# Sample's paged key scores four sequences at a time, with re-placed value buffers and five joined edits, in a two-layer hybrid decoder step

## The chip, the cores and the metric

The kernel is one program of several stages on one core of one Trainium2 chip. The metric is the device time of one execution in microseconds. TensorE (PE in the profile) multiplies and transposes; VectorE (DVE), ScalarE (ACT) and GpSimd (POOL) do the elementwise work; SyncE (SP) mostly asks for transfers. Each engine runs its own list of instructions in order, and they wait for one another on semaphores.

## The reference

Two layers run over 1024 prompt tokens and over 8 sample sequences of 4 new tokens each. The odd layer's sparse attention is the part that the change touches most. For a sample sequence it scores 8 query heads (in 2 key groups of 4) against the 1024 past keys, which lie in 8 pages of 128 keys, found by a page table:

```python
def _dsa_sample(q, k, v, qi, wi, ki, layer, cache_k, cache_v, cache_ik, page_table):
    ...
    kg = _paged_take(cache_k, layer, page_table, idx, k)
    vg = _paged_take(cache_v, layer, page_table, idx, v)
    return _sparse_attend(q, kg, vg, valid)
```

`_sparse_attend` is a masked softmax of q·k over the chosen keys times v. The kernel scores all keys and masks those that were not chosen. The even layer ends with a gMLP branch, `u * mixed * silu(gate)` for tiles of 128 tokens, and both layers end with an output projection that is added to the input.

## The kernel before

The stages follow one another: the even layer's front with its branches (0 to about 752 us), its output projection (to 917), the odd layer's front with indexer and selection (to 1522.75), and the odd layer's back, `layer1_back` (to the end). In each stage a plan, a list of slots written out by hand, sets the order: `follow` goes through the slots and, for each engine apart, advances the streams named in the slot by one step.

In `layer1_back` the streams are called in a slot in the order `smp`, `prep`, `job`, `ties` (for PE, `prep` issues the transposes of a block's queries and keys). `job` runs in slots 0 to 66: 64 jobs, one for each of 8 blocks of 128 prompt queries and 8 heads. A job is scores on PE (`scores`, `back_s` in the profile, up to 1024 keys wide, so 128 columns for the first eight jobs and 1024 for the last eight), mask and maximum on DVE (L4323), exponentials on ACT (L4203), transposes of the probabilities on PE (`all_banks`, L4060), their copy on ACT or DVE (L4198 on ACT), and the product with the values on PE (L4069). `prep` makes the queries and keys of block p (p = 2 is block 1 of the prompt and begins in slot 1; p = 3 to 8 are blocks 2 to 7 and begin in slots 6, 14, 22, 30, 38 and 46): ACT squares (L4156), DVE reduces (L4252), POOL takes the root and multiplies and rotates (L3874 and the lines after it), PE transposes (L3953).

`smp` is Sample. Slots 1 to 17 are its paged key scores, in 16 units. Unit u is four key pages of one sequence. SP asks for three of the four pages and POOL for the fourth, into a ring of four key buffers. PE transposes the pages of the two key groups (`turned`, L3968, eight transposes into the banks `bankX` and `bankZ`), ACT copies one bank (L4175) and DVE the other (L4273) to `skT`, a ring of two, and PE multiplies (`smp_scores`, L3980): two products of 512 columns with 128 stationary columns. `qz` is the queries laid out with zeros in all columns but the 32 of this sequence, so that four units add into one bank `bankY` without disturbing one another. After each four units DVE adds the mask rows (`ye`). In slot 18 the scores against the four new keys follow (L3997). The softmax over all of it and its transposes (L4008) come next, and from slot 23 on the products with the value pages (L4031), four matmuls a page. The value pages of eight sequences go through a ring of four buffers `vp`, asked for by POOL (b = 0 to 4 and 6) and SP (5 and 7); those of b = 4 and 5 may be asked for only when the products of the first pair of sequences are done (`pvd`).

POOL starts the stage with `minus` and `qz` cleared (L3856, L3858) and then asks for its key pages; ACT may lay out `qz` only after that (`made`, L4145). At a stage's end `clear` resets the stage's semaphores in barriers of all engines, one for each run of adjacent numbers (L84). In the output projections the fp32 weights are split into an upper part (ACT, L351) and the rest (DVE, L395), and PE takes three products for each piece. At the even layer's end DVE does `mixed` (L2163, four pieces) and `gated` (L2170) for each tile of the gMLP; u and the gate come back from memory (`gu`, `gg`), except the gate of the last tile, which is taken from the evacuation's buffer `st`. L1760 is the evacuation itself.

## Time and profile before

| | |
|---|---|
| three runs | 1963.12 us median, 1958.63 to 1963.51 |
| the profiled execution | 1961.93 us, span 1960.3 us, mean granted clock 0.972 |
| PE busy | 1823.4 us, 93% of the span |
| DVE, ACT, POOL busy | 975.5, 601.6, 421.3 us |
| `layer1_back`, 1522.75 to 1960.30 | 437.55 us, of which PE is busy 394.89 |

PE is busy for most of the time in every stage, so an edit can gain where PE waits or where it takes work from PE. The rows further down give the places. "Idle before" in square brackets is the time that the engine stood still ahead of a row, and what ended it.

### The profile page before, as it was taken

What the parts mean: (1) busy time and instruction counts of PE and PEld (TensorE: products, weight loads), DVE (VectorE), ACT (ScalarE), POOL (GpSimd) and SP (SyncE); (2) the same over time, 40 slices, a digit from 0 to 9 for tenths busy, and PEclk for the clock granted to TensorE, in tenths of its full rate; (3) what the DMA queues carried; (4) which work ended last, traced back from release to release, by engine and by line L of the source; (5) the groups of instructions that cost most, each with busy time, mean ns of one, the idle gap of its engine ahead of it and who ended that gap; (6) DMA issues with size and microseconds to landing.
All of it is one profiled execution on the core that took longest, in us unless ns stands there. A gap on an engine that the chain in (4) does not pass through costs nothing. (4 is left out here: it accounts for less than half of the span.)

```text
span 1960.3 us, 26802 instructions
## 1 busy us (share of the span) xinstructions
PE 1823.4 (93%) x9553; PEld 1407.4 (72%) x9553; DVE 975.5 (50%) x2274; ACT 601.6 (31%) x1273; POOL 421.3 (21%) x663
## 2 busy tenths in 40 slices
PE   7999999999999997998999898999989689899998
PEld 5666788777777885886876466787667466677887
DVE  5412643224466765123431567888776555575211
ACT  3111332111122113101211346787634345453000
POOL 4301222000133442000331001211004364430000
PEclk9999999998899998999999999999999899999999
DMA  6433333444344467122222121334243755323221
GB/s 210 136 108 113 104 109 108 157 159 126 105 140 155 127 201 292 76 101 79 65 66 69 42 71 61 113 100 148 99 144 90 233 171 151 123 87 98 105 113 44
DMA packets 128487, 235.15 MB, mean 120 GB/s; under 512 B 28354, under 2 KB 54370, under 8 KB 128354
## 3 DMA queue, kind: packets, MB, share of 16 engines
q1 hardware_dynamic: 109010, 170.63, 26.8%
q0 software_dynamic: 18144, 58.47, 9.5%
q10 hardware_dynamic: 1200, 4.33, 0.6%
q8 instruction: 77, 1.26, 0.3%
q14 instruction: 56, 0.46, 0.1%
HBM read 167.22 MB, written 66.16 MB: 119 GB/s over the span
## 5 line engine op out<-in xcount | busy, mean ns | idle before, releaser
L1170 PE MATMUL layer_acc<-layer_w_hi,layer_xT_hi 128*128 128x512 f32 x640 | 262.7, 410 | 0.2 <-PE all_banks L1318 0.2
L1172 PE MATMUL layer_acc<-layer_w_hi,layer_xT_lo 128*128 128x512 f32 x640 | 253.9, 397 | 0.0
L1171 PE MATMUL layer_acc<-layer_w_lo,layer_xT_hi 128*128 128x512 f32 x640 | 253.2, 396 | 0.0
L2726 PE MATMUL front_acc<-front_w_hi,front_xT_hi 128*128 128x512 f32 x520 | 221.3, 426 | 16.2 <-DVE front_st L3196 5.2
L2727 PE MATMUL front_acc<-front_w_lo,front_xT_hi 128*128 128x512 f32 x520 | 208.9, 402 | 0.0
L2728 PE MATMUL front_acc<-front_w_hi,front_xT_lo 128*128 128x512 f32 x520 | 208.6, 401 | 0.0
L1170 PEld LDWEIGHTS layer_acc<-layer_w_hi,layer_xT_hi 128*128 128x128 f32 x640 | 122.4, 191 | 30.6 <-issue 5.9
L1171 PEld LDWEIGHTS layer_acc<-layer_w_lo,layer_xT_hi 128*128 128x128 f32 x640 | 121.7, 190 | 26.8 <-issue 2.6
L1172 PEld LDWEIGHTS layer_acc<-layer_w_hi,layer_xT_lo 128*128 128x128 f32 x640 | 121.3, 189 | 27.0
L2726 PEld LDWEIGHTS front_acc<-front_w_hi,front_xT_hi 128*128 128x128 f32 x520 | 100.5, 193 | 49.5 <-issue 7.9
L3042 ACT ACTIVATE front_index_rows<-odd_bias,front_candidate 128x1024 bf16<-128x1024 f32 (+3 forms) x128 | 124.9, 981 | 14.3 <-DVE front_candidate L3336 9.3
L2728 PEld LDWEIGHTS front_acc<-front_w_hi,front_xT_lo 128*128 128x128 f32 x520 | 99.4, 191 | 23.7
L2727 PEld LDWEIGHTS front_acc<-front_w_lo,front_xT_hi 128*128 128x128 f32 x520 | 100.4, 193 | 17.2
L2554 POOL DMA_DIRECT2D all_w<-in_w_odd x57 | 32.7, 574 | 318.2 <-DVE front_w_lo L3244 120.3
L996 POOL DMA_DIRECT2D all_w<-in_w_even x80 | 44.7, 560 | 260.9 <-DVE layer_w_lo L109 139.5
L1526 ACT ACTIVATE layer_st<-layer_acc 128x512 f32<-128x512 f32 x48 | 28.7, 597 | 228.8 <-PE layer_acc L1172 222.5
L4069 PEld LDWEIGHTS all_banks<-back_v,back_first_scratch 128*128 128x128 f32 x576 | 73.6, 198 | 33.8 <-issue 25.8
L4069 PE MATMUL all_banks<-back_v,back_first_scratch 128*128 128x128 f32 x576 | 80.1, 286 | 17.9 <-issue 13.9
L1524 ACT ACTIVATE layer_st<-layer_acc 128x512 f32<-128x512 f32 (+1 forms) x36 | 21.5, 597 | 227.8 <-PE layer_acc L1172 224.5
L301 PE MATMUL out_acc<-out_w_hi,out_yT_hi 128*128 128x512 f32 x192 | 77.0, 401 | 11.7 <-DVE out_w_lo L395 11.7
L4203 ACT ACTIVATE back_first_scratch<-back_first_scratch,back_neg 128x128 f32<-128x128 f32 (+7 forms) x64 | 49.8, 779 | 109.3 <-DVE back_neg L4329 60.1
L4046 PE MATMUL back_s<-back_kT,back_first_scratch 128*128 128x512 f32 (+3 forms) x192 | 74.3, 497 | 8.3 <-ACT back_kT L4139 8.3
(661 smaller groups left out, 3680.8 us busy)
## 6 DMA issues: line engine op xcount, KB each, us to landing
all_w<-in_w_even POOLq DMA_DIRECT2D x80, 256.0 KB, 3.8
h_even<-layer_st SPq DMA_DIRECT2D x79, 256.0 KB, 2.1
all_w<-in_w_odd POOLq DMA_DIRECT2D x61, 256.0 KB, 3.6
h_odd<-front_st SPq DMA_DIRECT2D x56, 256.0 KB, 2.1
layer_scratch<-h_even SPq DMA_DIRECT2D x47, 256.0 KB, 3.0
all_scratch<-in_w_mem SPq DMA_DIRECT2D x32, 256.0 KB, 3.9
all_scratch<-h_even SPq DMA_DIRECT2D x32, 256.0 KB, 3.7
all_scratch<-x SPq DMA_DIRECT2D x14, 512.0 KB, 3.6
```

The source lines that it names most:

```text
L301: T.matmul(out, yh[u][:, k, :], wh[:, k, e], start=(k == 0), stop=False, skip_group_check=True)
L996: pool.dma_start(raw[n % RAW][:, :], a["w_even"][ORDER[chunk][0] // CW, :, CW * kk:CW * kk + CW]).then_inc(w_in[n % RAW], 16)
L1170: T.matmul(out[0:rows, :], xh[:, kk, to], wh[:, r, :], start=(kk == 0), stop=False)
L1171: T.matmul(out[0:rows, :], xh[:, kk, to], wl[:, r, :], start=False, stop=False)
L1172: ins = T.matmul(out[0:rows, :], xl[:, kk, to], wh[:, r, :], start=False, stop=(kk == KC - 1))
L2726: T.matmul(out[0:rows, :], xh[:, k, to], wh[:, r, :], start=(k == 0), stop=False, skip_group_check=True)
L2727: T.matmul(out[0:rows, :], xh[:, k, to], wl[:, r, :], start=False, stop=False, skip_group_check=True)
L2728: ins = T.matmul(out[0:rows, :], xl[:, k, to], wh[:, r, :], start=False, stop=(k == KC - 1), skip_group_check=True)
L3042: A(flags_at(i), rows_at(i), ACT.Sign, bias=cand[:, j:j + 1], scale=-1.0, accum_out=cnt[:, j:j + 1]).then_inc(ca, 1)
L4046: T.matmul(psS[:, 512 * (m % 2):512 * (m % 2) + n], qT[i % 2][:, h, :], kT[:, h // 4, k:k + n], start=True, stop=True)\
L4069: ins = T.matmul(bankO[:, 0:P], pT[g % 2][:, k, :], v[:, k, HD * (h // 4):HD * (h // 4) + HD], start=(k == 0), stop=(k == i))
L4203: A(y, y, ACT.Exp, bias=neg[g % 3][:, :], scale=SC, accum_out=tot[g % 4][:, :]).then_inc(ex, 1)
```

## The change

1. **Scores by four.** `smp_scores` runs only after the units 3, 7, 11 and 15, for four units at once: eight products, each with the 32 stationary columns of its own sequence, into four column tiles `bankY[32q:32q+32]`. `turned` still runs for every unit. The ring `skT` has six places.
2. **Pages.** SP asks for two key pages and POOL for two on even units (three and one on odd ones). Each of the eight value buffers has a place of its own until the fourth pair, where two places are used again. ACT now asks for the value pages of b = 0 and 1, one page at the end of each of the first 16 job slots; POOL asks for b = 2 in slots 13 to 16; b = 3, 4 and 5 are asked for in slots 17 to 20 by SP and POOL; b = 6 and 7 in slot 27 (the fifth w step), after the first pair's products. At the stage's start POOL asks for three key pages (units 2 and 3) before its memsets, SP asks for unit 2's pages and the first gate tile earlier, and eight small transfers of Sample's gate (`gs`) go from the start to slots 13 and 14. ACT copies the keys before the queries and lays out `qz` in slot 1.
3. **Prep later.** For p > 2 the DVE reduction and POOL's steps come one slot after ACT's square.
4. **Last output tile.** Its products run by halves of 512 columns; sum and store follow each half.
5. **One range.** The last stage clears its semaphores in one barrier.
6. **First weight piece.** In the even layer's output projection the first piece is split in two halves.
7. **gMLP's end.** The tile before the last (i = 7) also takes its gate from `st` and has its u loaded early, and DVE takes `mixed` 7, `gated` 7 and `mixed` 8 ahead of tile 6.

```diff
+    def clear_range(self):
+
+        self.nc.all_engine_barrier(sems_to_clear=range(min(self.nums), max(self.nums) + 1))
+
...
             def w_upper(k):
                 act.wait_ge(*w_there(k))
+                if k == 0:
+                    for e in halves:
+                        A(wh[:, k, e], w(k)[:, e], ACT.Copy).then_inc(whi, 1)
+                    return
                 A(wh[:, k, :], w(k), ACT.Copy).then_inc(whi, 1)
...
             def w_lower(k):
-                dve.wait_ge(whi, k + 1)
+                if k == 0:
+                    for n, e in enumerate(halves):
+                        dve.wait_ge(whi, n + 1)
+                        V.tensor_tensor(wl[:, k, e], w(k)[:, e], wh[:, k, e], ALU.subtract).then_inc(pieces, 1)
+                    return
+                dve.wait_ge(whi, k + 2)
                 V.tensor_tensor(wl[:, k, :], w(k), wh[:, k, :], ALU.subtract).then_inc(pieces, 1)
 
...
-        u_of = lambda i: X[:, 512:1024] if i == T1 - 1 else gu[i % 2]
+        u_of = lambda i: X[:, 512:1024] if i == T1 - 1 else S[:, 3072:3584] if i == T1 - 2 else gu[i % 2]
+        late_gate = lambda i: i >= T1 - 2
...
-                sp.wait_ge(gyd, i + 1)
+                sp.wait_ge(gyd, T1 - 1 if i == T1 - 3 else i + 1)
...
-                    if i == 6:
+                    if i == 5:
                         load_gu(T1 - 1)
+                        load_gu(T1 - 2)
...
                 u, rows = i % 2, rows_in(TILE[i])
-                gate = gg[u] if i < T1 - 1 else st[(UNITS - 1) % ST]
+                gate = st[(UNITS - T1 + i) % ST] if late_gate(i) else gg[u]
                 V.tensor_tensor(u_of(i)[0:rows, :], u_of(i)[0:rows, :], gate[0:rows, :], ALU.mult).then_inc(gyd, 1)
...
                 for i in range(T1):
-                    if i:
+                    if i == T1 - 2:
+                        mixed(T1 - 2)
+                        dve.wait_ge(*evacuated(UNITS - 2))
+                        gated(T1 - 2)
+                        mixed(T1 - 1)
+                    if 0 < i < T1 - 1:
                         mixed(i - 1)
                         gated(i - 1)
                     if i + 2 < T1:
                         norm(i + 2)
-                    if i == T1 - 1:
-                        mixed(T1 - 1)
                     yield
...
-        skT = [WH[:, 4096 + 1024 * u:5120 + 1024 * u].rearrange("p (n k) -> p n k", n=KVH) for u in range(2)]
+        skT = [(WH[:, 4096 + 1024 * u:5120 + 1024 * u] if u < 2 else WL[:, 2048 + 1024 * u:3072 + 1024 * u]).rearrange("p (n k) -> p n k", n=KVH)
+               for u in range(TRING)]
...
-        vp = [WL[:, 2048 * r:2048 * r + 2048].rearrange("p (g n) -> p g n", g=PAGES) for r in range(VRING)]
+        vp = [of[:, at:at + 2048].rearrange("p (g n) -> p g n", g=PAGES) for of, at in (
+            (WL, 0), (WL, 2048), (WH, 0), (WH, 2048), (WL, 4096), (WL, 6144), (WL, 0), (WL, 2048))]
+        by_pool = lambda u: (2, 3) if u % 2 == 0 else (3,)
...
+                load_last_k(2)
+                load_last_k(3)
                 G.memset(minus[:, :], -SC).then_inc(made, 1)
                 pool.wait_ge(made, 1)
                 G.memset(qz, 0.0).then_inc(made, 1)
-                load_last_k(2)
-                load_last_k(3)
...
-                        if step == 0:
+                        at = step - (p > 2)
+                        if at == 0:
                             pool.wait_ge(red, p - 1)
...
+                for p in by_pool(u):
+                    at = PAGES * seq_of(u) + 4 * hf + p
+                    page = pool.value_load(c.page_ids[0:1, at:at + 1], min_val=0, max_val=n_pool - 1)
+                    src = a["cache_attn_k"][0, bass.ds(page, 1)].rearrange("o s h d -> (o s) (h d)")
+                    pool.dma_start(kp[r][p], src).then_inc(kq_in[r], 16)
...
 
             def smps():
                 for u in range(UNITS + 6):
                     if u + KRING < UNITS:
                         load_last_k(u + KRING)
-                    if 2 <= u < UNITS + 2:
...
+                    pe.wait_ge(kp_in[r], 16 * (4 - len(by_pool(u))) * loads)
+                    pe.wait_ge(kq_in[r], 16 * len(by_pool(u)) * loads)
                 else:
-                    pe.wait_ge(qcp, 2)
+                    pe.wait_ge(qcp, 3)
...
-            def smp_scores(u):
-                gr, hf, q = unit(u)
-                pe.wait_ge(kca, u + 1)
-                pe.wait_ge(kcd, u + 1)
-                if u == 0:
+            def smp_scores(m):
+                pe.wait_ge(kca, 4 * m + 4)
+                pe.wait_ge(kcd, 4 * m + 4)
+                if m == 0:
                     pe.wait_ge(qcp, 6)
-                if q == 0:
-                    pe.wait_ge(ye, u // 4)
+                pe.wait_ge(ye, m)
                 for n in range(KVH):
-                    ins = T.matmul(bankY, qz[:, n, seq_of(u), :], skT[u % 2][:, n, :], start=(q == 0 and n == 0), stop=(q == 3 and n == 1),
-                                   skip_group_check=True)
+                    for q in range(4):
+                        u, e = 4 * m + q, slice(32 * q, 32 * q + 32)
+                        ins = T.matmul(bankY[e, :], qz[:, n, seq_of(u), e], skT[u % TRING][:, n, :], start=(n == 0), stop=(n == 1),
+                                       skip_group_check=True)
                 ins.then_inc(sc2, 1)
...
@@ -4170,9 +4223,9 @@
             def smps():
                 for u in range(UNITS):
                     act.wait_ge(ktr, 2 * u + 1)
-                    if u >= 2:
-                        act.wait_ge(sc2, u - 1)
-                    A(skT[u % 2][:, 0, :], bankX, ACT.Copy).then_inc(kca, 1)
+                    if u >= TRING:
+                        act.wait_ge(sc2, (u - TRING) // 4 + 1)
+                    A(skT[u % TRING][:, 0, :], bankX, ACT.Copy).then_inc(kca, 1)
...
+                    if g < 2 * PAGES:
+                        b, p = divmod(g, PAGES)
+                        act.dma_start(vp[b][:, p, :], value_page(act, b, p)).then_inc(va_in[b], 16)
                     yield
...
-                        if step == 0:
+                        if step == (0 if p == 2 else 1):
                             dve.wait_ge(squ, p - 1)
                             link(V.tensor_reduce(ssq[u][0:rows, :], heads(sq[0:rows, :], H10), AX.X, ALU.add))
...
-                            dve.wait_ge(sc2, u - 1)
-                        V.tensor_copy(skT[u % 2][:, 1, :], bankZ).then_inc(kcd, 1)
+                        if u >= TRING:
+                            dve.wait_ge(sc2, (u - TRING) // 4 + 1)
+                        V.tensor_copy(skT[u % TRING][:, 1, :], bankZ).then_inc(kcd, 1)
                     if u and u % 4 == 0:
                         gr, hf, _ = unit(u - 1)
-                        dve.wait_ge(sc2, u)
+                        dve.wait_ge(sc2, u // 4)
...
+                if j == T1 - 1:
+                    for n, e in enumerate(HALVES):
+                        dve.wait_ge(mm, j + n + 1)
+                        V.tensor_tensor(x[u][:, e], psS[:, e], x[u][:, e], ALU.add).then_inc(add, 1)
+                    return
```

The next two excerpts are PE's program in the units 3 and 4 of Sample (`back_first_smp` and `all_w` are the key pages; in the L3980 row and in the L4022 row `back_first_smp` is the turned keys and `qz`). Before:

```order
L3980 MATMUL back_x<-back_first_smp 128x512 x2
L4069 MATMUL all_banks<-back_v,back_first_scratch 128x128
L4060 MATMUL all_banks<-all_ident,back_first_scratch 128x128
L4046 MATMUL back_s<-back_kT,back_first_scratch 128x128
L3968 MATMUL back_x<-all_ident,back_first_smp 128x128 x4
L3968 MATMUL all_banks<-all_ident,back_first_smp 128x128 x4
L3980 MATMUL back_x<-back_first_smp 128x512 x2
L4069 MATMUL all_banks<-back_v,back_first_scratch 128x128
L4060 MATMUL all_banks<-all_ident,back_first_scratch 128x128
L4046 MATMUL back_s<-back_kT,back_first_scratch 128x128
```

And PE in the same slots after the change:

```order
L4010 MATMUL back_x<-all_ident,back_first_smp 128x128 x4
L4010 MATMUL all_banks<-all_ident,back_first_smp 128x128 x4
L4113 MATMUL all_banks<-back_v,back_first_scratch 128x128
L4104 MATMUL all_banks<-all_ident,back_first_scratch 128x128
L4090 MATMUL back_s<-back_kT,back_first_scratch 128x128
L4010 MATMUL back_x<-all_ident,all_w 128x128 x4
L4010 MATMUL all_banks<-all_ident,all_w 128x128 x4
L4022 MATMUL back_x<-back_first_smp 32x512 x8
L3995 MATMUL all_banks<-all_ident,all_scratch 128x128 x4
L4113 MATMUL all_banks<-back_v,back_first_scratch 128x128
L4104 MATMUL all_banks<-all_ident,back_first_scratch 128x128
L4090 MATMUL back_s<-back_kT,back_first_scratch 128x128
```

The two products of 512 columns that followed each unit's eight transposes are gone, and eight products with 32 stationary columns stand once behind four units.

The following two are POOL's program at the start of `layer1_back` (each TENSOR_LOAD reads a page number, each DMA asks for one key page). Before:

```order
L3856 MEMSET back_minus_scale 128x1
L3858 MEMSET back_first_smp 128x2048
L3895 TENSOR_LOAD odd_pages
L3895 ISA x2
L3897 ISA
L3897 DMA back_first_smp<-in_cache_attn_k 128x256
L3895 TENSOR_LOAD odd_pages
L3895 ISA x2
L3897 ISA
L3897 DMA back_first_smp<-in_cache_attn_k 128x256
L3862 MEMSET back_own 128x16
L3866 MEMSET back_own 32x1 x8
```

And POOL at that place after the change:

```order
L3938 TENSOR_LOAD odd_pages
L3938 ISA x2
L3940 ISA
L3940 DMA back_first_smp<-in_cache_attn_k 128x256
L3938 TENSOR_LOAD odd_pages
L3938 ISA x2
L3940 ISA
L3940 DMA back_first_smp<-in_cache_attn_k 128x256
L3938 TENSOR_LOAD odd_pages
L3938 ISA x2
L3940 ISA
L3940 DMA back_first_smp<-in_cache_attn_k 128x256
L3899 MEMSET back_minus_scale 128x1
L3901 MEMSET back_first_smp 128x2048
```

The memset of `qz` (128x2048) now stands behind three page requests instead of ahead of the first.

The last two are DVE's program at the end of the even layer (L1760 evacuates, L2163 is `mixed`, L2170 `gated`, 17 lines further down in the changed file). Before:

```order
L1760 SCALAR_TENSOR_TENSOR layer_st<-layer_st,layer_acc 128x512
L2163 SCALAR_TENSOR_TENSOR layer_scratch<-layer_a,layer_bs,layer_scratch 128x128 x4
L2170 TENSOR_TENSOR layer_scratch<-layer_scratch 128x512
L1760 SCALAR_TENSOR_TENSOR layer_st<-layer_st,layer_acc 128x512
L2163 SCALAR_TENSOR_TENSOR layer_scratch<-layer_a,layer_bs,layer_scratch 128x128 x4
L2170 TENSOR_TENSOR layer_scratch<-layer_scratch 128x512
L2163 SCALAR_TENSOR_TENSOR all_scratch<-all_banks,layer_bs,all_scratch 128x128 x4
L2170 TENSOR_TENSOR all_scratch<-all_scratch,layer_st 128x512
```

And DVE after the change:

```order
L2180 SCALAR_TENSOR_TENSOR layer_scratch<-layer_a,layer_bs,layer_scratch 128x128 x4
L2187 TENSOR_TENSOR layer_scratch<-layer_scratch,layer_st 128x512
L2180 SCALAR_TENSOR_TENSOR all_scratch<-all_banks,layer_bs,all_scratch 128x128 x4
L2180 SCALAR_TENSOR_TENSOR layer_scratch<-layer_a,layer_bs,layer_scratch 128x128 x4
L2187 TENSOR_TENSOR layer_scratch<-layer_scratch 128x512
L1777 SCALAR_TENSOR_TENSOR layer_st<-layer_st,layer_acc 128x512
L2187 TENSOR_TENSOR all_scratch<-all_scratch,layer_st 128x512
```

The last evacuation now has one multiplication of 128x512 behind it, where it had two groups of `mixed` and two of `gated`.

## Rows read from the trace of the kernel before

**Rows 1.** The page's busy times: engine, us, share of the span, instructions.
```profile
PE 1823.4 (93%) x9553; PEld 1407.4 (72%) x9553; DVE 975.5 (50%) x2274; ACT 601.6 (31%) x1273; POOL 421.3 (21%) x663
```

**Rows 2.** Windows: length, PE, PEld, DVE, ACT, POOL busy, PE clock, DMA share, GB/s.
```profile
1524.10:1543.70 19.60, 13.54 (x61) 9.56 (x61) 9.95 (x25) 7.02 (x34) 8.95 (x21) 0.85 0.93 314
1543.70:1574.50 30.80, 25.09 (x113) 16.27 (x113) 24.51 (x64) 11.34 (x30) 13.54 (x15) 0.88 0.68 202
1574.50:1604.10 29.60, 27.17 (x144) 18.46 (x144) 14.05 (x47) 12.71 (x32) 17.09 (x26) 1.00 0.60 184
```

**Rows 3.** Timeline of PE, slots 1 to 18: start, length, row, idle before.
```profile
1532.43 0.66 PE L3968 MATMUL back_x<-all_ident,back_first_smp 128*128 128x128 f32 x4 [2.01 <-DMA back_first_smp<-in_cache_attn_k]
...
1574.55 0.63 PE L3968 MATMUL back_x<-all_ident,back_first_smp 128*128 128x128 f32 x4 [1.60 <-ACT back_first_smp L4175]
...
1575.45 1.88 PE L3980 MATMUL back_x<-back_first_smp 128*128 128x512 f32 x4
1577.17 0.61 PE L4069 MATMUL all_banks<-back_v,back_first_scratch 128*128 128x128 f32 x4
...
1604.06 3.63 PE L3997 MATMUL back_x<-back_kT,back_first_smp 128*128 128x4 f32 x32
```

**Rows 4.** Timeline of PE in the even layer, a group in column tiles.
```profile
352.54 0.64 PE L1318 MATMUL all_banks<-layer_scratch 128*32 128x256 f32 x8
```

**Rows 5.** Timeline at the start of `layer1_back`, POOL, ACT and DVE.
```profile
1522.90 1.81 POOL L3858 MEMSET back_first_smp<- 128x2048 f32 x1
...
1524.74 1.34 ACT L4145 ACTIVATE back_first_smp<-all_banks 128x16 f32<-128x16 f32 x16 [0.61 <-POOL back_first_smp L3858]
...
1528.22 1.49 DVE L4252 TENSOR_REDUCE all_scratch<-all_scratch 128x10 f32<-128x1280 f32 x1 [0.81 <-ACT all_scratch L4156]
...
1537.03 0.55 POOL L3907 DMA_DIRECT2D back_first_smp<-in_cache_attn_v  x1 [0.60 <-PE all_banks L3968]
...
1541.70 0.35 DVE L4339 SCALAR_TENSOR_TENSOR all_mem_keysT<-all_banks,back_rec,all_mem_keysT 128x128 f32<-128x128 f32 x1 [4.13 <-DMA all_mem_keysT<-h_odd]
```

**Rows 6.** Groups of instructions of DVE and of ACT, 1524 to 1605 us.
```profile
L4273 DVE COPY back_first_smp<-all_banks 128x512 f32<-128x512 f32 x16 | 11.1, 691 | 7.7 <-PE all_banks L3968 6.9 <-DVE odd_bias L4360 0.4
L4175 ACT ACTIVATE back_first_smp<-back_x 128x512 f32<-128x512 f32 x16 | 9.4, 590 | 2.4 <-PE back_x L3968 2.4
```

**Rows 7.** Timeline of PE where the value products wait, and after.
```profile
1669.78 0.63 PE L4031 MATMUL back_x<-back_first_smp 128*16 128x128 f32 x16 [3.61 <-DMA back_first_smp<-in_cache_attn_v]
1670.34 2.10 PE L4069 MATMUL all_banks<-back_v,back_first_scratch 128*128 128x128 f32 x10
...
1675.99 1.28 PE L4069 MATMUL all_banks<-back_v,back_first_scratch 128*128 128x128 f32 x10
```

**Rows 8.** Timeline of PE and DVE where a block is prepared.
```profile
1627.05 1.20 PE L4069 MATMUL all_banks<-back_v,back_first_scratch 128*128 128x128 f32 x4 [2.97 <-issue]
...
1651.55 1.49 DVE L4252 TENSOR_REDUCE all_scratch<-all_scratch 128x10 f32<-128x1280 f32 x1 [1.20 <-ACT all_scratch L4156]
...
1718.82 2.90 PE L4069 MATMUL all_banks<-back_v,back_first_scratch 128*128 128x128 f32 x12 [2.29 <-issue]
```

**Rows 9.** Timeline of DVE at the even layer's end.
```profile
745.93 0.69 DVE L1760 SCALAR_TENSOR_TENSOR layer_st<-layer_st,layer_acc 128x512 f32<-128x512 f32 x1 [2.09 <-ACT layer_st L1524]
748.08 1.13 DVE L2163 SCALAR_TENSOR_TENSOR layer_scratch<-layer_a,layer_bs,layer_scratch 128x128 f32<-128x128 f32 x4 [1.46 <-DMA layer_scratch<-h_even]
...
751.00 0.69 DVE L2170 TENSOR_TENSOR all_scratch<-all_scratch,layer_st 128x512 f32<-128x512 f32 x1
```

**Rows 10.** Timeline of DVE, the first weight piece of the output projection.
```profile
755.55 1.23 DVE L395 TENSOR_TENSOR out_w_lo<-all_scratch,out_w_hi 128x1024 fp32r<-128x1024 f32 x1 [0.25 <-ACT out_w_hi L351]
```

**Rows 11.** Timeline of DVE, the last sum.
```profile
1953.51 1.23 DVE L4388 TENSOR_TENSOR all_scratch<-back_s,all_scratch 128x1024 f32<-128x1024 f32 x1 [15.10 <-PE back_s L4117]
```

**Rows 12.** Waits of SP's queue, 1945 to 1961 us: sum, times, longest.
```profile
SPq L84 <- PEq L84: 2.0, 3, 0.8
```

**Rows 13.** Timeline of ACT, its own page requests' nearest relative.
```profile
798.08 1.46 ACTq L356 DMA_DIRECT2D x<-all_scratch  x2
```

158 lines of the change are left out of this document (90 added, 68 removed).

## The prediction

> **What bounds it now.** I read the page's busy times first: PE is busy for 93% of the span [rows 1], so a gain is either work taken from PE or a place where PE stands still. Then the table by stretch, which shows where that is. In the 80.0 us of Sample's paged scores PE is busy 13.5 of 19.6, 25.1 of 30.8 and 27.2 of 29.6 us [rows 2]. Each stretch has its own limit. In the second DVE is busy 24.5 of 30.8 us, and PE's clock was granted at 0.85 and 0.88. In the third PE itself is full, at full clock. Last, PE's timeline says who ends its waits: key pages at 1532.43, ACT's copy at 1574.55 [rows 3], value pages for 3.61 us at 1669.78 [rows 7], and the copy behind a block's preparation (up to 2.97 us, released by nothing that the profile names) at 1627.05 and 1718.82 [rows 8].
>
> **What an edit of PE's work is worth.** One unit's two products begin at 1575.45 and the next work at 1577.17: 1.72 us, and 1.88 to their own end, so 0.16 of draining [rows 3]. Sixteen units are 27.5 us. For column tiles the nearest row is the even layer's: four products of 256 columns in tiles of 32 take 0.64 us [rows 4]. One after the other the same 1024 columns are the 1.88 us of a unit. Less the drain that is 0.48 against 1.72, so tiles run 3.6 times as fast, nearly side by side. Eight products of 512 columns are then two rounds of 0.86 plus about 0.14, **1.85 us**; if the shorter product's overhead doubles with its length, 2 x 2 x 0.48 = 1.9 and the drain, 2.1; if tiles don't overlap, 8 x 0.86 = 6.9. Four calls at 1.85 are 7.4, so PE loses 20.1 us of work (0 where tiles don't overlap). The Trainium skill ("TensorE: Matmul & The Clock Gate", Measured speedup vs the span model) gives 2.38 times for three column tiles of 512; for four at that efficiency an estimate is 3.2 times, 2.2 us a call, which would make the sum smaller by at most 1.3 us.
>
> **Slots 1 to 17, -12.5 us.** Not all 20 us come out, because PE isn't the limit everywhere.
> - *Start.* POOL now makes three page requests ahead of the memset of 1.81 us. A request is 0.55 us and 0.60 of reading the page number, 1.15 [rows 5], so the memset ends 3.45 later. ACT's layout of `qz` (1.34) waits for it, the square stands behind that, and DVE's reduction, now at 1528.22, comes at 1531.7 at the latest. On the other side PE's wait of 2.01 us for pages at 1532.43 [rows 3] goes.
> - *Up to `turned(10)`, now at 1574.55.* DVE has 9.95 + 24.51 = 34.5 us of work in these two stretches [rows 2]. Laid end to end from 1531.7 it is done at 1566.2. About 2.8 us of it is exchanged for waits that the chain mask, exponential, transposes, sum keeps: **1569**, a gain of 5.5. The wait of 4.13 us at 1541.70 for the gate tile [rows 5] ends because SP asks for it first; it is part of the slack that these 5.5 use up. The bounds are 0 (the late start eats it all) and 8.3 (no waits).
> - *Slots 11 to 17.* From 1574.55 to 1604.06 are 29.5 us with seven units' products [rows 3]. Seven go (12.0) and two calls of 1.85 come: 21.2. ACT is busy 12.71 there and now has up to seven page requests; DVE 14.05, POOL 17.09 [rows 2]. A request by ACT is 0.73, from 1.46 for two [rows 13], so ACT has 17.8 of 21.2 us. It fits, closely. I give 1.4 us back for places where ACT or POOL is late, so Sample's last scores come at **1591.5** and not 1604.06. Bounds -5 and -20 (all of PE's work).
> - *Copies.* ACT's copy of a unit takes 0.59 and DVE's 0.69 us [rows 6], the same number as before. The ring of six lets them run ahead, which costs nothing and saves no time of theirs.
>
> A rule speaks against the size of this. The Trainium skill ("TensorEngine Tiling (Array Packing)", PSUM Bottleneck) says that after a fourfold speedup of TensorE the copy out of PSUM may become the limit. By it the gain would stay at some 3 us; that case stands among the rivals, worked out from rows.
>
> **Value pages, -5.4.** Before, POOL and SP could ask for sequences 4 and 5 only after the first pair's products, and PE stood 3.61 us at 1669.78. Behind this wait the same ten products took 2.10 us where they take 1.28 a little later [rows 7], which is PE's clock at half; with the transposes and scores of that slot in the same ratio this is about 1.8. Now pages of 4 and 5 are asked for in slots 17 to 20, far ahead, and those of 6 and 7 in slot 27, with the second, third and more slots of other work over them. What hides them is the jobs of a slot, over 4 us each; without that cover a pair is the 3.61 again. Bounds -3.6 and -6.
>
> **Prep later, -5.5.** DVE waits for ACT's square (1.20 us at 1651.55, then 1.49 for the reduction [rows 8]), and the job's mask stands behind it, so PE idles. There are four such slots (22, 30, 38, 46): the first idles PE 2.97, the last 2.29, and the last one's products then run 2.90 us at a lower clock [rows 8]. With the square a slot earlier the 1.2 or more of DVE's wait goes each time and the 1.49 of the reduction stays: four times about 1.2, and 0.7 for the clock. What is late next is POOL, whose rotation must be ready for PE's transposes at step 6: it begins one slot later with the same room behind, about a slot. Bounds -2 and -10.
>
> **Even layer's end, -4.3.** DVE's last evacuation is done at 745.93 + 0.69 = 746.6, then it waits 1.46 for u and gate of tile 7 and ends at 751.69 [rows 9]. Now only one multiplication of 0.69 stands behind the evacuation: 747.3. The stage change follows DVE, so 4.4; I take 4.3. If stores or PE take over, 3; bounds -3 and -4.8.
>
> **First piece, -1.0.** DVE's half of 1.23 [rows 10] is 0.69, as 128x512 rows of DVE are [rows 9], so 0.54; ACT's copy ahead of it is halved too, an estimate of 0.45. Bounds 0 and -1.2.
>
> **Tail, -1.9.** The last sum of 1.23 [rows 11] ends in a half of 0.69, 0.54 less. Of the barriers' 2.0 us in three waits [rows 12] a third stays, 1.3 less. Bounds -1.2 and -2.6.
>
> **The sum.** 12.5 + 5.4 + 5.5 + 4.3 + 1.0 + 1.9 = 30.6. Against the profiled execution's 1961.93 that is 1931.3; its own time lies 1.2 below the runs' median 1963.12, so I forecast **1932.5 us** for the median.
>
> **Rivals.**
> - *Chain-bound slots (0.12).* The hand-overs of a job between PE, DVE and ACT, with the copies of 0.59 and 0.69, set the slots and not PE's work. Then the first ten slots gain nothing and slots 11 to 17 give 3: 12.5 becomes 3, **1942**. For it: DVE 24.5 of 30.8. Against: PE 27.2 of 29.6 in the third stretch [rows 2].
> - *Tiles don't overlap (0.07).* Eight products cost 6.9. Slots 11 to 17 gain nothing and the first part half: some 2, **1943**. Against it stands the 0.64 [rows 4].
> - *More (0.05).* DVE's waits vanish, the clock comes up from 0.85 and 0.88, and the four prep slots lose all their idle time: slots 1 to 17 give 18, prep 9: 1923, and less with each bound.
> - *Slower (0.04).* ACT's 16 page requests, with an address from a register, are dear. ACT is busy 31.1 us in the 80.0 [rows 2], and everything in its list waits behind a request. With price p its work is 31.1 + 16p. The other terms give 18.1, so it decides above 98.1 us, p = 4.2. At p = 5 it is 111.1, 31.1 more than now: **1976**. For it: nothing here shows such a request by ACT. Against it: two plain ones take 1.46 [rows 13], and POOL's, with the page number, 1.15 each [rows 5].
> - *No change (0.02).* All these places are hidden by something that I don't see, and the late start takes the rest: 1963.
>
> **How the numbers follow.** The forecast has 0.70. Its own terms' bounds give 1920 to 1948; not all ends come together, so 1922 to 1943. With chain-bound slots and tiles that don't overlap, whose own spread reaches 1946, the range is **1920 to 1946**. Within 0.3% (6 us, about what a measurement of this kernel can tell from none) is 1957 to 1969: faster 0.94, same 0.02, slower 0.04.
>
> **What would show it.** the scores against the four new keys (L3997 before) at about 1586 us on the profile's clock (1591.5 less the 5.3 gained in the stages before) and not 1604; the row of eight products at some 2 us; ACT's requests under 1 us; no wait of L4031 for value pages; the stage `layer1_back` near 412 us where it is 437.55; PE's idle time in slots 22, 30, 38 and 46 at half or less; DVE's last row of the even layer ending near 747. I would be wrong if DVE or ACT shows as the releaser of PE in slots 11 to 17, or if PE's transposes of a block wait for POOL's rotation.

## The result and the profile after

The changed kernel takes 1934.43 us (median of 4 runs, 1932.26 to 1936.03), the one before 1961.13 (4 runs, 1958.63 to 1963.51). The ratio is 0.9863, 95% interval 0.9846 to 0.9879: 26.7 us less. The forecast was 1932.5 us, worked out as 30.6 less than the profiled execution; the two profiled executions differ by 29.6 in span (1930.7 against 1960.3). The sum came out, but partly by chance: its largest term came to half, another was too small, and 1.9 us came from stages that nothing touched.

The windows of the changed kernel over the same three stretches of Sample's scores, counted from the stage's first ACT row (columns as in [rows 2]):

```profile
1517.50:1537.10 19.60, 10.63 (x49) 9.54 (x48) 9.42 (x23) 6.64 (x32) 9.70 (x21) 0.56 0.95 329
1537.10:1567.30 30.20, 20.14 (x122) 13.37 (x123) 24.89 (x66) 12.39 (x32) 12.32 (x13) 0.80 0.64 198
1567.30:1594.20 26.90, 25.07 (x177) 19.74 (x178) 14.62 (x50) 13.36 (x34) 15.69 (x21) 0.91 0.74 232
```

PE does less in the first two (10.6 and 20.1 us where [rows 2] has 13.5 and 25.1), and its clock fell from 0.85 and 0.88 to 0.56 and 0.80. PE's timeline there, with the rows that answer to [rows 3]:

```profile
1523.21 1.09 PE L4010 MATMUL back_x<-all_ident,all_w 128*128 128x128 f32 x4 [3.17 <-ACT back_first_smp L4228]
1524.09 1.06 PE L4010 MATMUL all_banks<-all_ident,all_w 128*128 128x128 f32 x4
1529.55 1.09 PE L4010 MATMUL back_x<-all_ident,back_first_smp 128*128 128x128 f32 x4 [3.76 <-ACT back_first_smp L4228]
...
1540.86 3.64 PE L4022 MATMUL back_x<-back_first_smp 128*32 128x512 f32 x16
...
1558.41 1.92 PE L4022 MATMUL back_x<-back_first_smp 128*32 128x512 f32 x16
...
1567.25 1.09 PE L4010 MATMUL back_x<-all_ident,back_first_smp 128*128 128x128 f32 x4 [4.21 <-ACT back_first_smp L4228]
...
1590.84 3.63 PE L4040 MATMUL back_x<-back_kT,back_first_smp 128*128 128x4 f32 x32
```

The eight products in column tiles take 1.92 us, as sized (1.85), and 3.64 where the clock is at half (1.2 instead of 2.4 GHz). A group of four transposes takes 1.06 instead of 0.60 for the same reason. The waits of PE from 1517 to 1800 us name who ends them (us in total, times, longest):

```profile
PE back_x L4010 <- ACT back_first_smp L4228: 16.2, 7, 4.2
...
PE all_banks L4113 <- ACT back_first_scratch L4251: 6.2, 8, 1.6
PE all_banks L4113 <- issue: 3.9, 3, 1.8
```

In the same view of the kernel before, PE waited 3.6 us for that copy; now 16.2. No value page is among the releasers (3.61 in [rows 7]). What ACT does ahead of such a copy, on its timeline:

```profile
1527.70 0.40 ACT L4256 ACTIVATE back_first_scratch<-back_first_scratch,back_neg 128x128 f32<-128x128 f32 x1 [2.15 <-DVE back_neg L4383]
1528.01 0.19 ACT L4256 ACTIVATION_READ_ACCUMULATOR back_first_scratch<-back_first_scratch,back_neg 128x1 f32 x1
1528.40 0.36 ACTq L4266 DMA_DIRECT2D back_first_smp<-in_cache_attn_v  x1
1528.81 0.60 ACT L4228 ACTIVATE back_first_smp<-back_x 128x512 f32<-128x512 f32 x1 [0.61 <-issue]
```

The exponential waits for DVE's mask, then comes the page request, and only then the copy: 0.61 us of standing still, and PE's transposes at 1529.55 wait behind it.

DVE's timeline has at the even layer's end the rows that answer to [rows 9] and [rows 10], and at the start of the last stage its first mask:

```profile
746.45 0.69 DVE L1777 SCALAR_TENSOR_TENSOR layer_st<-layer_st,layer_acc 128x512 f32<-128x512 f32 x1 [2.55 <-ACT layer_st L1541]
747.17 0.69 DVE L2187 TENSOR_TENSOR all_scratch<-all_scratch,layer_st 128x512 f32<-128x512 f32 x1
...
751.38 1.28 DVE L405 TENSOR_TENSOR out_w_lo<-all_scratch,out_w_hi 128x512 fp32r<-128x512 f32 x2
...
1520.60 0.29 DVE L4379 CUSTOM_DVE_ANT_0 back_first_scratch<-back_s,odd_bias 128x128 f32<-128x128 f32 x1 [7.99 <-POOL back_minus_scale L3899]
...
1545.68 0.35 DVE L4395 SCALAR_TENSOR_TENSOR all_mem_keysT<-all_banks,back_rec,all_mem_keysT 128x128 f32<-128x128 f32 x1 [0.33 <-DVE back_rec L4390]
```

PE's timeline has the first product behind them:

```profile
752.21 0.77 PE L305 MATMUL out_acc<-out_w_hi,out_yT_hi 128*128 128x512 f32 x1 [6.43 <-DVE out_w_lo L405]
```

And SP's waits at the kernel's end answer to [rows 12]:

```profile
SPq L77 <- PEq L77: 1.1, 1, 1.1
```

DVE ends the even layer at 747.86 (751.69 in [rows 9]). Its first mask in the last stage waits for POOL's small memset, which now stands behind three page requests. And the wait of 4.13 us for the gate tile [rows 5] is gone: the same row at 1545.68 waits for no transfer.

**A measure that is steadier than the total.** Between two marks that no edit moves in any run, from the first product of the even output projection to the first ACT row of `layer1_back`, the runs took 762.0 to 768.4 us. The first mark scatters too: 749.9 to 755.0 us in the eleven traces with the changed even layer, 756.9 to 757.6 in the three without. So I read the stage by itself: times from its first ACT row to DVE's copy of unit 10 (the eleventh), to Sample's scores against the new keys, and to the last job's reciprocal on DVE, each worked out from timeline rows. The same code in three runs gave 53.0, 52.9 and 53.1 us, then 74.7, 74.5 and 74.6, and in two runs 253.1 and 253.0 for the last. The ratios are against executions of the kernel before taken beside each group of runs, whose medians are in its row.

| kernel | unit 10 | new scores | last job | median of runs | ratio to before, interval |
|---|---|---|---|---|---|
| before | 52.9 | 81.3 | 273.7 | 1961.13 to 1962.64 | |
| changed | 53.0 | 74.7 | 253.1 | 1934.43 | 0.9863, 0.9846 to 0.9879 |
| page request before exponential | 50.6 | 71.3 | 251.0 | 1931.87 | 0.9847, 0.9816 to 0.9878 |
| scores of each unit | 49.2 | 76.3 | 255.8 | 1936.23 | 0.9875, 0.9843 to 0.9907 |
| POOL's memsets first | 51.9 | 73.7 | 253.8 | 1932.15 | 0.9848, 0.9822 to 0.9874 |
| preparation together | 55.2 | 81.0 | 270.7 | 1953.45 | 0.9951, 0.9928 to 0.9974 |
| units, then fours | 49.0 | 69.3 | 249.0 | 1932.93 | 0.9855, 0.9827 to 0.9884 |
| before, preparation later | 48.9 | 81.3 | 267.9 | 1956.79 | 0.9967, 0.9945 to 0.999 |
| value pages late | 53.1 | 74.6 | 259.3 | 1941.9 (one run) | |
| ends as before | 52.9 | 74.5 | 253.0 | 1940.21 | 0.9885, 0.9858 to 0.9912 |
| first pages by POOL | 49.0 | 78.0 | 260.6 | 1941.69 | 0.9898, 0.9868 to 0.9927 |
| useless products | 49.7 | 70.1 | 249.7 | 1930.09 | 0.9845, 0.9808 to 0.9882 |
| fours late, small memset first | 48.3 | 68.2 | 249.2 | 1929.52 | 0.9841, 0.9814 to 0.9869 |
| first pages by SP | 49.8 | 75.2 | 254.7 | 1935.1 | 0.9865, 0.9838 to 0.9892 |

(In the expectations below, "to the transposes of unit 10" was read from PE's rows, about 1 us ahead of DVE's copy. The 48.1 of products of each unit is that row; the 52.4 named for the run with the request moved is the row of unit 11, and that of unit 10 is 49.5.)

### The profile page after: what moved, and what is told of

Read it like the earlier page. It is cut to its first block and busy times, and to the rows that moved or that the text cites. A ratio compares the mean times of both kernels' runs of the same rounds, so it can differ in the third digit from the quotient of the medians.

```text
span 1930.7 us, 26765 instructions
## 1 busy us (share of the span) xinstructions
PE 1802.3 (93%) x9553; PEld 1396.5 (72%) x9553; DVE 977.6 (51%) x2276; ACT 602.7 (31%) x1274; POOL 412.5 (21%) x646
## 5 line engine op out<-in xcount | busy, mean ns | idle before, releaser
L1189 PE MATMUL layer_acc<-layer_w_hi,layer_xT_lo 128*128 128x512 f32 x640 | 253.8, 397 | 0.0
L1189 PEld LDWEIGHTS layer_acc<-layer_w_hi,layer_xT_lo 128*128 128x128 f32 x640 | 121.4, 190 | 27.1
L4113 PEld LDWEIGHTS all_banks<-back_v,back_first_scratch 128*128 128x128 f32 x576 | 71.3, 194 | 23.7 <-issue 13.0
L4256 ACT ACTIVATE back_first_scratch<-back_first_scratch,back_neg 128x128 f32<-128x128 f32 (+7 forms) x64 | 49.7, 776 | 97.2 <-DVE back_neg L4385 56.2
```

The lines of the kernel that those rows point to most:

```text
L1189: ins = T.matmul(out[0:rows, :], xl[:, kk, to], wh[:, r, :], start=False, stop=(kk == KC - 1))
L4113: ins = T.matmul(bankO[:, 0:P], pT[g % 2][:, k, :], v[:, k, HD * (h // 4):HD * (h // 4) + HD], start=(k == 0), stop=(k == i))
L4256: A(y, y, ACT.Exp, bias=neg[g % 3][:, :], scale=SC, accum_out=tot[g % 4][:, :]).then_inc(ex, 1)
```

## The experiments

**ACT's request ahead of the exponential.**

```diff
+                    if g < 2 * PAGES:
+                        b, p = divmod(g, PAGES)
+                        act.dma_start(vp[b][:, p, :], value_page(act, b, p)).then_inc(va_in[b], 16)
                     if g < JOBS:
                         exps(g)
-                    if g < 2 * PAGES:
-                        b, p = divmod(g, PAGES)
-                        act.dma_start(vp[b][:, p, :], value_page(act, b, p)).then_inc(va_in[b], 16)
```

> The changed kernel with ACT's value-page request moved ahead of the job's exponential, where ACT waits for DVE's mask anyway. Theory: in slots 1 to 10 a chain goes round once per slot, from PE's scores over DVE's mask, ACT's exponential and ACT's copy of the turned keys (L4228, for which PE waits 16.2 us in 7 waits) back to PE's next transposes, and the request (0.6 to 0.85 us between exponential and copy) lies in it. Then some 7 x 0.6 = 4 us come out between the stage's first ACT row and Sample's last scores (74.7 us now, about 71 then), and the kernel takes about 1930 us. Rival: ACT comes too late for the mask anyway, so the place of the request is worth nothing and the stretch stays within 1 us of 74.7.

New scores 3.4 us earlier, the last job 2.1. On ACT the copy now starts 0.40 us after its exponential (1529.75 and 1530.15), where it was 1.11. The request was in the chain; the theory held.

**Products of each unit.** `smp_scores` as before the change, all else as changed.

```diff
-                    if u % 4 == 3:
-                        smp_scores(u // 4)
+                    smp_scores(u)
```

> The changed kernel with the products of each unit as before, two of 512 columns with 128 stationary ones after each unit's transposes; everything else of the change stays (ring of six, pages, start). Theory: the first ten slots are bound by the chain through DVE and ACT, so that the 1.72 us of products are hidden there (0 to 1 us), and slots 11 to 17 by PE, where 7 x 1.72 - 2 x 1.92 = 8.2 us of work come back and about 6 of it shows. In all 6 to 7 us slower than the changed kernel, the stretch to Sample's last scores 81 us instead of 74.7. Rival A: PE's work is what binds in all slots, then 4 x (4 x 1.72 - 1.92) = 20 us. Rival B: the chain binds in all slots and the gain there came from the pages and the ring, then 0 to 2 us.

Neither the theory's 6 to 7 nor rival A: 1.6 us later at the new scores, 2.7 at the last job (by DVE's reciprocals 4.6 from the 19th to the 46th job; that 1.9 come back at the 47th I did not follow up). The 1.6 lies in rival B's range, but not for its reason, since PE's work does bind in slots 11 to 17. With 20 us more of products on PE in all 16 units the first ten slots are 3.8 us *shorter* (49.2 against 53.0), and from there to the new scores it is 27.1 against 21.7. The first two windows of this kernel:

```profile
1516.70:1536.30 19.60, 14.47 (x61) 9.99 (x60) 10.33 (x25) 7.20 (x34) 9.70 (x21) 0.73 0.96 329
1536.30:1566.50 30.20, 24.72 (x124) 16.26 (x125) 25.25 (x68) 13.13 (x35) 15.11 (x18) 0.97 0.73 223
```

The clock is at 0.73 and 0.97 where fours have 0.56 and 0.80.

**POOL's memsets first.**

```diff
+                G.memset(minus[:, :], -SC).then_inc(made, 1)
+                pool.wait_ge(made, 1)
+                G.memset(qz, 0.0).then_inc(made, 1)
                 load_last_k(2)
                 load_last_k(3)
-                G.memset(minus[:, :], -SC).then_inc(made, 1)
-                pool.wait_ge(made, 1)
-                G.memset(qz, 0.0).then_inc(made, 1)
```

> The changed kernel with POOL's two memsets ahead of its three key page requests, as before the change. DVE's first mask waits for the first memset now and starts 4.4 us after the stage's first ACT row, 2.4 before the change. Theory: this late start is carried into the chain of the first slots and costs 1 to 2 us, so 1 to 2 us faster than the changed kernel. Rival: the key pages of unit 2 then come late and PE waits up to 2.0 us for them as before the change, so nothing is gained or 1 us lost.

1.0 us at the new scores, given back by the last job (0.7 later). The order at the start is worth nothing in the end.

**Preparation together again.**

```diff
-                        at = step - (p > 2)
+                        at = step
...
-                        if step == (0 if p == 2 else 1):
+                        if step == 0:
```

> The changed kernel with DVE's reduction and POOL's steps of a block's preparation in the same slot as ACT's square, as before the change. Theory: the four slots 22, 30, 38 and 46 lose again what the two traces show as gained there, 3.2 + 1.6 + 1.1 + 2.7 = 8.6 us, and slots 6 and 14 some tenths: 7 to 9 us slower than the changed kernel. The forecast had 5.5 for it. Rival: most of these steps came from other edits (gate transfers moved, value pages asked for elsewhere), then 0 to 3 us.

17.6 us in the stage, 17 by the two ratios: twice the theory and three times the forecast. 6.3 of it is there at the new scores already. DVE's reciprocals, one for each job, say where: 7.8 us are lost by the 18th job, that is with blocks 2 and 3, whose preparation begins in slots 6 and 14, and 9.8 in the four slots behind (4.5, 1.6, 1.0 and 2.7). PE's waits in this kernel, 1520 to 1790 us:

```profile
PE back_x L4010 <- ACT back_first_smp L4228: 15.5, 8, 3.8
PE all_banks L4113 <- issue: 15.3, 7, 3.0
```

The waits of the jobs' value products that nothing in the profile ends ("issue") are 15.3 us where the changed kernel has 3.9 (13.9 before).

**Units first, then fours**, with the request moved.

```diff
-                    if u % 4 == 3:
-                        smp_scores(u // 4)
+                    if u < 8:
+                        smp_scores(u)
+                    elif u % 4 == 3:
+                        smp_scores_of_four(u // 4)
```

> The kernel with ACT's page request ahead of the exponential, and the products of units 0 to 7 as before (each unit by itself, 128 stationary columns), of units 8 to 15 by fours in column tiles. Theory after the first four runs: with the products gone PE does so little in the first ten slots that its clock is granted lower (0.56 and 0.80 of full speed in the two stretches with fours, 0.73 and 0.97 with each unit's products), the transposes take 1.06 instead of 0.60 us, and the chain gets longer by what PE's other work loses. Then both halves are had: the first ten slots as with each unit (48.1 us from the first ACT row to the transposes of unit 10, or a little less by the moved request), then 23.6 us as with fours: Sample's last scores 68 to 71 us after the first ACT row, where the fours with the moved request took 71.3 and the changed kernel 74.7. In all 2 to 5 us faster than the changed kernel. Rival: the clock has nothing to do with it, the extra 8 x 1.72 us of PE work cost what they cost, and the stretch is 73 us or more.

69.3 us to the new scores, as expected: 5.3 us before the changed kernel. 4.1 of it arrive at the last job.

**The kernel before, preparation later.** The two edits of the fourth run the other way round, in the kernel before.

> The kernel before with one part of the change alone: DVE's reduction and POOL's steps of a block's preparation one slot after ACT's square, for p > 2. Undoing this in the changed kernel cost 17.6 us of the stage. Theory: it is worth about as much by itself, since the square's wait stands in front of a job's mask on DVE whatever else is done: 10 to 17 us faster than before. Forecast: 5.5 us faster. Rival: in the kernel before, other waits take its place (gate tile, value pages), then 0 to 3 us.

5.7 us in the stage and 5.8 in the medians (2 to 11 by the interval): near the forecast's 5.5, and not the theory's 10 to 17. Up to unit 10 it gains 4.0, and all of that is lost by the new scores. PE's row in slot 12 says where:

```profile
1581.99 1.12 PE L3954 MATMUL all_banks<-all_ident,all_scratch 128*128 128x128 f32 x4 [4.14 <-POOLq L3888]
```

PE waits 4.14 us for POOL's rotation of block 2. The step that is moved later runs into POOL's page requests. So the 5.7 is a difference: by DVE's reciprocals this kernel is 1.8 us behind at the 18th job, and gains 7.6 behind it, where the four slots lie that the forecast priced. Sample's value pages still keep PE waiting, only earlier: 3.86 us at 1656.03, where the kernel before waits 3.61 at 1669.78.

**Value pages late.**

```diff
-                    if UNITS <= u < UNITS + 4:
-                        load_v(4, range(2 * (u - UNITS), 2 * (u - UNITS) + 2))
...
                     if w == 4:
                         pool.wait_ge(pvd, 1)
-                        load_v(6, range(PAGES))
+                        load_v(4, range(PAGES))
+                    if w == 8:
+                        load_v(6, range(PAGES))
```

> The changed kernel with the value pages of sequences 4 and 5 asked for only after the products of the first pair, those of 6 and 7 four slots later, as before the change (POOL and SP as now, places as now). Theory: PE waits for them again for some 3.6 us before the third pair's products and then runs at a lower clock for a slot: 5 us more between the 32nd and the 34th job's end (7.4 us now, 12.7 before the change). Rival: POOL has less to do in those slots than before, so the pages are asked for earlier and the wait is under 1 us.

The last job comes 6.2 us later, and PE waits again ahead of the value products:

```profile
PE back_x L4073 <- issue: 3.8, 1, 3.8
```

The cost stands between the jobs 27 and 33 rather than at the 33rd, since the stage is ahead by then (0.6 us at the 17th job); the size is the forecast's (5.4, bounds 3.6 to 6), a little above.

**Ends as before.** Even layer's end, first piece, last tile and clearing undone together (their hunks of the diff reversed).

> The changed kernel with the even layer's end, the split first weight piece, the last output tile by halves and the one-range clearing undone. Theory: the first product of the even layer's output projection starts 4.7 us later (756.9 instead of 752.2), and the time behind the last job grows by 2.5 us (163.9 instead of 161.4): 7.2 us in all. Between the two traces 1.9 us more were gained in the stages from 752 to 1516 us, in which nothing was changed; the rival to chance is that this hangs on the earlier start, and then it is 9 us.

The first product of the output projection starts at 757.6 us (752.2 changed, 756.9 before), and the time behind the last job is 162.9 (161.4 and 163.9). That is 5.4 and 1.5 us. The 5.4 is a difference of single traces; the means of the eleven and the three traces named above differ by 4.9. Of the tail's 1.5, the last sum is 0.5 (1.22 against 0.69), the landing of the last store 0.6 (SP waits 2.2 against 1.6) and the barriers 0.3 (1.4 in three waits against 1.1 in one). The rest of the 2.5 is for the most part scatter of these barriers, which took 2.0 us in the kernel before and 1.6 in the run with its preparation later. The stages between took 768.4 us, the most of all runs, so the 1.9 gained there between the first two traces don't hang on an earlier start: they lie inside the scatter.

**First pages by POOL.**

```diff
+                    if 2 <= u < 10:
+                        b = (u - 2) // 4
+                        for p in range(2 * ((u - 2) % 4), 2 * ((u - 2) % 4) + 2):
+                            pool.dma_start(vp[b][:, p, :], value_page(pool, b, p)).then_inc(va_in[b], 16)
```

> The changed kernel with the 16 value pages of sequences 0 and 1 asked for by POOL, two a slot in slots 3 to 10, as before the change, and not by ACT. Theory: the later preparation gained only 5.7 us in the kernel before and 17.6 in the changed one, because POOL, busy with page requests, was late with a block's rotation (PE waited 4.1 us for it in slot 12). With the requests back on POOL this wait returns: 3 to 5 us of waiting for POOL ahead of block 2's transposes, against 0.6 to 0.85 us for each request that leaves ACT's list, which was 3.4 us up to Sample's last scores. So the last scores come 0 to 3 us later than in the changed kernel (74.7 us). Rival: POOL keeps up, because it has no pages in the slots behind, and the stretch is 3 us shorter (71.5).

The wait returned, and larger than expected:

```profile
1576.79 1.12 PE L3999 MATMUL all_banks<-all_ident,all_scratch 128*128 128x128 f32 x4 [8.11 <-POOLq L3929]
```

Up to unit 10 the stage is 4.0 us faster (ACT is free of requests, of which 2.4 us are known from the first run), 3.3 later at the new scores, and 7.5 later at the end.

**Useless products.**

```diff
+                    if u in (1, 2, 5, 6):
+                        if u == 1:
+                            pe.wait_ge(qcp, 6)
+                        pe.wait_ge(ye, u // 4)
+                        for n in range(KVH):
+                            T.matmul(bankY, qz[:, n, seq_of(u), :], skT[u % TRING][:, n, :], start=(n == 0), stop=(n == 1), skip_group_check=True)
                     if u % 4 == 3:
```

> The changed kernel with ACT's page request ahead of the exponential (all scores by fours), and with useless work added on PE: in the slots of units 1, 2, 5 and 6 two products of 512 columns into bankY, whose result the products by fours overwrite (4 x 1.72 us, with no new wait for ACT or DVE). The outputs are the same. Theory of the clock: what PE loses in the first ten slots with fours is its clock, so useless work brings it up from 0.59 and 0.84 and costs nothing: 48 to 51 us to the transposes of unit 10, where the same kernel without it took 52.4. Rival (order): with each unit's products the chain was shorter for another reason, the clock is a bystander, and useless work costs 0 to 7 us.

0.9 us earlier at unit 10 and 1.2 at the new scores and at the last job than the same kernel without them, for 7.6 us of work more: 2.48 from the first product's start to the next row, and 1.72 for each of the other three. The edit does add waits, in unit 1 for ACT's layout of `qz` and in unit 5 for DVE's mask rows, and is faster in spite of them. By PE's rows unit 10's transposes start 1.8 us earlier (47.7 against 49.5); the forecast's 48 to 51 was set against the row of unit 11, so it proves nothing. PE's timeline around the first two of them (L4037):

```profile
1530.11 2.65 PE L4037 MATMUL back_x<-back_first_smp 128*128 128x512 f32 x4
...
1533.15 0.60 PE L4010 MATMUL back_x<-all_ident,back_first_smp 128*128 128x128 f32 x4
1533.58 0.60 PE L4010 MATMUL all_banks<-all_ident,back_first_smp 128*128 128x128 f32 x4
1534.02 1.88 PE L4037 MATMUL back_x<-back_first_smp 128*128 128x512 f32 x4
...
1539.23 1.92 PE L4022 MATMUL back_x<-back_first_smp 128*32 128x512 f32 x16
```

And without them:

```profile
1533.67 1.06 PE L4010 MATMUL back_x<-all_ident,back_first_smp 128*128 128x128 f32 x4
1534.53 0.92 PE L4010 MATMUL all_banks<-all_ident,back_first_smp 128*128 128x128 f32 x4
...
1542.19 3.50 PE L4022 MATMUL back_x<-back_first_smp 128*32 128x512 f32 x16
```

So the clock is a cause and no bystander: behind the first useless product PE's rows run at full clock, and what the products cost is less than what they give back. The clock does not stay up throughout: unit 10's transposes take 1.09 us here and 0.63 in the kernel without them.

**Small memset first**, on top of units then fours.

```diff
+                G.memset(minus[:, :], -SC).then_inc(made, 1)
                 load_last_k(2)
                 load_last_k(3)
-                G.memset(minus[:, :], -SC).then_inc(made, 1)
                 pool.wait_ge(made, 1)
```

> The kernel with units 0 to 7 by themselves, units 8 to 15 by fours and the page request moved, and in addition POOL's small memset (0.12 us), for which DVE's first mask waits, ahead of the three page requests. Theory: DVE's first mask starts 2 us earlier and 0.5 to 1 us of it reaches Sample's last scores (69.3 us without): 68.3 to 68.8, and the kernel takes about 1930 us. Rival: ACT's layout of qz still waits for the large memset, so nothing is gained.

68.2 us to the new scores, 1.1 better; nothing of it at the last job (249.2 against 249.0). Its median is the lowest of all, 1929.52, 4.9 below the changed kernel's; the two intervals overlap, and the steadier measure gives 4.0 us less than changed.

**First pages by SP.** As the last run, but SP asks for the first 16 value pages, one in each of slots 1 to 16.

> As the run before it, with the value pages of sequences 0 and 1 asked for by SP (one in each of slots 1 to 16) and none by ACT. Theory: ACT's request already lies in ACT's waiting time, so taking it away gives 0 to 1 us; SP asks for key pages in the same slots and may make them up to 1 us late. Within 1 us of the run before. Rival: ACT's list is still a part of the chain in the full slots, then 2 to 4 us faster.

A miss for both: 7.0 us later at the new scores, 5.6 at the last job. PE waits for SP's key pages instead:

```profile
PE back_x L4013 <- DMA back_first_smp<-in_cache_attn_k: 2.8, 1, 2.8
```

Behind this wait PE's transposes take 1.11 us, and its clock over the second stretch (30.2 us) is 0.85 where the run before has 0.94. Wait and clock were not separated.

## Why the prediction was right in sum, and where it was wrong

The span fell by 29.6 us. By the stage's marks it divides so, with the forecast behind it: up to the new scores 6.6 (12.5), the slot of the value pages 5.3 (5.4), the rest of the stage 8.6 (preparation, 5.5), first product of the output projection 4.7 (5.3), tail 2.5 (1.9), and 1.9 in stages that nothing touched (none). The sum agrees because 5.9 too much in the first term meets 3.1 too little in the preparation and 1.9 of scatter; that is luck.

- **Slots 1 to 17, the step that failed.** "Laid end to end from 1531.7 it is done at 1566.2 ... a gain of 5.5": DVE's work does not lie end to end, and up to unit 10 nothing was gained (53.0 against 52.9). What binds there is a ring of hand-overs once per slot, scores on PE, mask on DVE, exponential and copy on ACT, transposes on PE.
- **What worked in the first ten slots.** By single edits, the later preparation takes 2.2 us out (4.0 in the kernel before), the page request on ACT puts 2.4 in, products by fours 3.8, and the late memset 1.1. These do not add up: with the request moved and the fours used only from unit 8 on, the stretch is 49.0, 4.0 shorter and not 6.2; beside the moved request (50.6) the fours cost only 1.6. The wait of 4.13 us for the gate tile went, which stands against them; no run undid that alone. With fours PE's clock falls, and transposes and scores at half clock take almost twice as long; that this is a cause is shown by the useless products, which gave 0.9 back although they are 7.6 us of work themselves. That all of the fours' cost is the clock is argued, not shown. What made the 6.6 us up to the new scores is then for the most part not the products, whose undoing costs 1.6 there, but the later preparation, with 6.3.
- **Why the forecast missed it.** It read 0.85 and 0.88 beside PE's busy time and did not ask what less work would make of them; it saw a clock coming up only as a case of more gain. The request was asked whether it fits ACT's busy time (17.8 of 21.2 us), and should have been asked what stands behind it. The rival of chain-bound slots was right for the first ten slots, and its 3 us too low for the rest.
- **The marks it named.** The new scores start at 1590.8 us (about 1586 forecast), `layer1_back` takes 414.5 (near 412), the even layer's last row on DVE ends at 747.86 (near 747), ACT's requests take 0.36 (under 1), and no value page is waited for.
- **Slots 11 to 17** were right in time: forecast 21.2 and 1.4 of friction, from unit 10's copy to the new scores 21.7 us, 28.4 before. But ACT is the releaser of PE there, which the forecast named as a sign of being wrong: 4.21 us at 1567.25, at the start of that stretch, and 1.7 in three short waits behind it.
- **The tiles** were right: 1.92 us against 1.85. At full clock four units' products were 4 x 1.72 = 6.9 us; eight in tiles are 1.92, or some 1.8 without the drain, nearly four times as fast. An estimate by the Trainium skill ("TensorE: Matmul & The Clock Gate", Measured speedup vs the span model) had 2.2 us; the trace has less. Its rule that the copy out of PSUM may become the limit after such a speedup ("TensorEngine Tiling (Array Packing)", PSUM Bottleneck) names the right releaser, ACT's copy with 16.2 us of PE's waits; but the copy itself is 0.60 long as before, and what made it late stands in front of it in ACT's list.
- **Preparation.** The forecast sized it for the kernel before and for slots 22 to 46. There it gains 7.6, and loses 1.8 ahead of them, so 5.7 against 5.5 is again partly luck. In the changed kernel undoing it costs 17.6, 9.8 in the four slots and 7.8 with blocks 2 and 3, which begin in slots 6 and 14 and which the forecast put at nothing without a reason. The parts are not additive: by itself it is held back by POOL ("what is late next is POOL", said the forecast, and gave it a slot of room: there was none in slot 12, 4.14 us). The page requests on ACT, which look like a cost, take POOL out of the way: undoing that costs 7.5. So the parts undone one by one are 17.6 + 7.5 + 6.2 + 2.7 = 34 us in a stage that gained 20.6.
- **Value pages, ends, first piece and tail** came within their bounds, the first product of the output projection by single traces that scatter by up to 5 us. For the value pages undoing gives 6.2, a little over the bound of 6. In the tail the barriers gave 0.9 where 1.3 was forecast, and the halved last store takes 0.6 less to land, which was not priced.
- **The slower rival** (dear requests on ACT) was far off: 0.35 us on the queue and about 0.6 of standing still, where 4.2 was the point of decision.

What stays open: how much of the fours' cost in the first ten slots is the clock, what the gate tile and the key pages by turns are worth alone, and how the 5.6 us of pages asked for by SP divide between waits and clock.

## What to carry to other kernels

A term of work taken from an engine counts only where that engine binds; in a chain of hand-overs ask for each instruction what stands behind it in its list, and for PE what its clock does when it has less to do. Work in column tiles belongs where PE is full, and where PE waits for others, the plain form may be free. An edit that acts in six places needs a price for each of the six. Parts of one change are priced in each other's presence: one that loads an engine off the path can be what lets another pay, so undo them one at a time from the finished kernel, and one at least alone on the old one.

## What the runs showed of the hardware

Useless matmuls made a stage faster. With 7.6 us of products that nobody reads, the granted clock of the two first windows went from 0.59 and 0.84 to 0.64 and 0.92 and the stage got 1.2 us shorter. Here are the two windows of the kernel without them, then of the kernel with them:

```profile
1520.04:1539.64 19.60, 10.60 (x50) 9.65 (x50) 10.61 (x25) 7.21 (x34) 9.70 (x21) 0.59 0.95 336
1539.64:1569.84 30.20, 21.24 (x133) 14.43 (x134) 24.52 (x67) 12.44 (x33) 13.87 (x16) 0.84 0.69 198
1517.50:1537.10 19.60, 13.39 (x58) 10.29 (x58) 10.56 (x25) 7.37 (x34) 9.70 (x21) 0.64 0.97 332
1537.10:1567.30 30.20, 22.11 (x144) 15.59 (x144) 24.75 (x69) 12.72 (x34) 15.11 (x18) 0.92 0.71 223
```

Eight fp32 products with 32 stationary columns, issued round the four column tiles, take 1.92 us at full clock; one after the other they would take 6.9, an estimate from the 1.72 us of two.
